# Three low parts of weights and one of an activation change engine or place at the borders of a Mamba2 mixer

## What is computed

```
hx = modulate(rmsnorm(x, pre_norm[l, 0]), mx[0], mx[1])       # scale and shift by column
z, xbc, dt_raw = jnp.split(h @ w_in, ...)                     # mixer in: xs, b, c, z, dt
xbc = silu(dwconv1d(xbc, conv_w, conv_b))
acs = cumsum(dt * a)                                          # by chunk, both directions
y = (y + d_skip * xs) * silu(z); y = y * rsqrt(mean(y * y) + EPS)
y = y * norm_w; out = y @ w_out                               # mixer out
x = x + mx[2] * rmsnorm(out, post_norm[l, 0])
hx = modulate(rmsnorm(x, pre_norm[l, 1]), mx[3], mx[4])       # and so to the FFN
x = x + mx[5] * rmsnorm((silu(conv(hx @ w_a)) * (hx @ w_v)) @ w_down, post_norm[l, 1])
```

## Time and profile before

| what | value |
|---|---|
| time of the kernel, median of 3 runs | 1337.94 us (1337.78 to 1338.17) |
| time of the profiled execution | 1337.82 us |
| its span in the profile | 1336.1 us |
| PE busy | 1297.3 us (97%), with the matmuls of `stay_busy` in it |
| DVE busy | 876.5 us (66%) |
| ACT busy | 656.1 us (49%) |
| POOL busy | 334.4 us (25%) |
| mean granted clock of the PE | 0.998 |

### The profile page before, as it was taken

How to read it: one execution, slowest core, us unless ns; L and a number is a source line. 1 busy time by engine, 2 the same in 40 slices (tenths; PEclk the granted TensorE clock), 3 DMA queues, 4 the chain that set the end, 5 groups by cost and what they waited for, 6 DMA issues and landing times. The chain is left out here.

```text
span 1336.1 us, 22159 instructions
## 1 busy us (share of the span) xinstructions
PE 1297.3 (97%) x8454; PEld 1093.4 (82%) x8454; DVE 876.5 (66%) x1717; ACT 656.1 (49%) x1037; POOL 334.4 (25%) x236
## 2 busy tenths in 40 slices
PE   5999999999999999999999999999999999999997
PEld 2678888887767888888888867899898879899997
DVE  4678777777697644222445778777777877774675
ACT  4445544445356433322333365555555645674664
POOL 1000000000203755105553030210111230683772
PEclk9999999999999999999999999999999999999999
DMA  9643444335470632234324334533333348366753
GB/s 345 202 142 123 131 132 137 127 118 167 158 244 23 190 95 87 71 110 123 98 71 134 103 126 111 158 95 95 95 95 94 95 157 255 110 200 173 219 164 111
DMA packets 274794, 183.28 MB, mean 137 GB/s; under 512 B 6642, under 2 KB 249106, under 8 KB 274706
## 3 DMA queue, kind: packets, MB, share of 16 engines
q1 hardware_dynamic: 274162, 180.00, 44.7%
q10 hardware_dynamic: 544, 2.10, 0.4%
HBM read 181.03 MB, written 1.05 MB: 136 GB/s over the span
## 5 line engine op out<-in xcount | busy, mean ns | idle before, releaser
L2218 PE MATMUL bank<-hh,wh 128*128 128x512 f32 (+1 forms) x1298 | 456.3, 352 | 3.5 <-DVE wl L1394 1.6
L2220 PE MATMUL bank<-hh,wl 128*128 128x512 f32 (+1 forms) x1298 | 451.6, 348 | 0.0
L2219 PE MATMUL bank<-hl,wh 128*128 128x512 f32 (+1 forms) x1298 | 451.2, 348 | 0.0
L849 ACT ACTIVATE wh<-wraw 128x1024 fp32r<-128x1024 f32 (+2 forms) x265 | 256.9, 985 | 84.0 <-PE bank L2220 59.4
L2218 PEld LDWEIGHTS bank<-hh,wh 128*128 128x128 f32 x1298 | 244.0, 188 | 39.1 <-DVE wl L1394 3.5
L1868 DVE SCALAR_TENSOR_TENSOR conv<-bank,pv,conv 128x189 f32<-128x189 f32 (+3 forms) x396 | 172.4, 436 | 152.9 <-ACT conv L1126 138.0
L2220 PEld LDWEIGHTS bank<-hh,wl 128*128 128x128 f32 x1298 | 243.9, 188 | 32.5
L1394 DVE TENSOR_TENSOR wl<-wraw,wh 128x1024 fp32r<-128x1024 f32 (+2 forms) x171 | 192.9, 1149 | 116.9 <-ACT wh L849 116.9
L2219 PEld LDWEIGHTS bank<-hl,wh 128*128 128x128 f32 x1298 | 244.1, 188 | 30.1
L737 POOL TENSOR_TENSOR wl<-wraw,wh 128x1024 fp32r<-128x1024 f32 (+2 forms) x87 | 198.8, 2291 | 197.3 <-ACT wh L849 197.0
L783 POOL TENSOR_TENSOR hl<-yT,hh 128x512 fp32r<-128x512 f32 x13 | 19.5, 1522 | 352.8 <-DVE gates L1764 340.3
(11 more groups left out here) (354 smaller groups left out, 2069.0 us busy)
## 6 DMA issues: line engine op xcount, KB each, us to landing
wraw<-in_ffn_w_up SPq DMA_DIRECT2D x88, 512.0 KB, 3.9
araw<-in_ada_w SPq DMA_DIRECT2D x40, 1024.0 KB, 8.2
wraw<-in_mb_w_in SPq DMA_DIRECT2D x48, 512.0 KB, 4.0
wraw<-in_hg_w_in SPq DMA_DIRECT2D x40, 512.0 KB, 3.9
wraw<-in_ffn_w_down SPq DMA_DIRECT2D x32, 512.0 KB, 4.0
wraw<-in_mb_w_out SPq DMA_DIRECT2D x16, 512.0 KB, 4.8
gates<-in_ada_w SPq DMA_DIRECT2D x5, 1024.0 KB, 9.3
wraw<-in_hg_w_out SPq DMA_DIRECT2D x8, 512.0 KB, 4.2
```

The costliest lines, as they stand in the source:

```text
L849: act.activation(slot(whp, n, 0, size), wraw[:, n % SLOTS, 0:size], ACT.Copy).then_inc(w_hi, 1)
L2218: pe.matmul(dst, W, hi(k), start=(k == 0), stop=False, **skip)
L2219: pe.matmul(dst, W, lo(k), start=False, stop=False, **skip)
L2220: ins = pe.matmul(dst, L, hi(k), start=False, stop=(k == nk - 1), **skip)
```

## The change

It has four parts.

1. The low part of `b 0` at border one is made by POOL (`part(at["b", 0])`, between `split_rest(0, T)` and `norm_low(1, T)`) instead of by DVE behind tile 1.
2. The low part of `xs 1 1` is made by DVE right behind the six scans of `dt_sums`, instead of behind all of `dt_sums`.
3. At the mixer's end DVE copies `yt 7` instead of ACT, with `tensor_scalar`, and makes the last tile's low part instead of POOL. The copies stand ahead of `gate_scales(1, 0)`, the low part behind it.
4. The low part of `up 1 0 1 1` at border two is made by POOL, between `y_low(1, ...)` and `norm_low(2, SEQ)`, instead of by DVE behind tile 1.

```diff
--- before.py
+++ after.py
@@ -432,7 +432,7 @@
         if g == MB_GROUPS + 1:
             plan.add(("am", LATE + 9), 6, "act")
         if Q:
-            mkey(("yt", q), "act")
+            mkey(("yt", q), "act" if q < MB_GROUPS - 1 else "dve")
         if S:
             mkey(("off", p, 0), "dve")
             mkey(("off", p, 1), "dve")
@@ -492,7 +492,7 @@
             for c in range(nf):
                 for part in range(2):
                     sub(("up", l, half, c, part), SUB, P, cols(a["ffn_w_up"][l], 0, KT, part * FF + (f0 + c) * P, P),
-                        ffp[l, half, "up"][0] + 2 * c + part + 1, "dve" if half == 0 and 2 * c + part < 5 - l or by_vector(l, half, c, part) else "pool")
+                        ffp[l, half, "up"][0] + 2 * c + part + 1, "dve" if half == 0 and 2 * c + part < 5 - 2 * l or by_vector(l, half, c, part) else "pool")
             for m in range(KT):
                 done = plan.index[("fy", l, m)][0] if half else ffp[l, 0, "down"][0] + m + 1
                 for j, (k0, nk) in enumerate(((0, KT), (KT, nf - KT))):
@@ -507,7 +507,7 @@
     for g in range(MB_GROUPS):
         for i in range(2):
             sub(("xs", g, i), SUB, P, cols(m_in, 0, KT, XS0 + (2 * g + i) * P, P), ("xs", g, i))
-        sub(("b", g), SUB, P, cols(m_in, 0, KT, B0 + g * P, P), ("b", g))
+        sub(("b", g), SUB, P, cols(m_in, 0, KT, B0 + g * P, P), ("b", g), "dve" if g else "pool")
         sub(("c", g), SUB, P, cols(m_in, 0, KT, C0 + g * P, P), ("c", g))
         for i in range(2):
             sub(("z", g, i), SUB, 256, cols(m_in, 4 * i, 4, 256 * g, 256), ("z", g))
@@ -801,6 +801,7 @@
         y_low(0, range(2, KT - 1))
         norm_low(0, T)
         split_rest(0, T)
+        part(at["b", 0])
         norm_low(1, T)
 
         pool.wait_ge(x_new, KT + 1)
@@ -828,7 +829,8 @@
             pool.wait_ge(skc_ready, g + 1)
             pool.tensor_tensor(hd(skip[:, :, :], 2), hd(xtok[:, 0:2, :], 2),
                                skc[:, :, :].unsqueeze(3).to_broadcast([P, 2, 4, HD]), ALU.mult).then_inc(scaled_ready, 1)
-        y_low(1, range(KT))
+        y_low(1, range(KT - 1))
+        part(at["up", 1, 0, 1, 1])
         norm_low(2, SEQ)
         split_rest(1, SEQ)
 
@@ -1329,7 +1331,7 @@
                 split_hi(at["z", g, 0] + 3)
             if g == MB_GROUPS + 1:
                 ada_rows(LATE + 9)
-            if Q:
+            if 0 <= q < MB_GROUPS - 1:
                 key = ("yt", q)
                 plan.wait_ready(act, key)
                 yk = yT[:, :, :].rearrange("p a b -> p (a b)")
@@ -1484,7 +1486,7 @@
             step.wait()
             V.tensor_scalar(ssx[:, 0:n], ssx[:, 0:n], 0.0, None, ALU.max).then_inc(var_ready, 1)
 
-        def add_and_norm(l, s, n, rows, weight=None):
+        def add_and_norm(l, s, n, rows):
 
             i = 2 * l + s
             first, second = ("r", l, s), ("r2", l, s)
@@ -1530,8 +1532,6 @@
                     plan.empty(ins, "dve", second)
                 if m < KT - 1 and (m == 0 or n == T):
                     turn(m + 1)
-                if m == 1 and weight is not None:
-                    split_lo(weight)
             hhn[0] += KT
 
         xn, rn, norms = [0], [0], [0]
@@ -1942,7 +1942,7 @@
         psum_freed_dve = plan.freed["dve"]
         ffn_dve(0, T, True)
         variance(0, 1, T, at["b", 0] - 1)
-        add_and_norm(0, 1, T, LATE + 5, at["b", 0])
+        add_and_norm(0, 1, T, LATE + 5)
 
         u, e, w = dtw[:, 0, :], dtw[:, 1, :], dtw[:, 2, :]
 
@@ -1985,6 +1985,7 @@
                         step(ins)
                     ends.append((r, slice(lo, hi), hi - 1 if d == 0 else lo))
             ins.then_inc(dt_dve, 1)
+            split_lo(at["xs", 1, 1])
             dve.wait_ge(dt_dve, 3)
             for r, c, last in ends:
                 step(V.tensor_scalar(elf[r, c], atf[r, c], -1.0, atf[r, last:last + 1], ALU.mult, ALU.add))
@@ -2151,7 +2152,8 @@
                 if g == 0:
                     ada_add(LATE + 6)
                     dt_sums()
-                split_lo(at["z", g, 0] + 3)
+                else:
+                    split_lo(at["z", g, 0] + 3)
             if S:
 
                 for d in range(2):
@@ -2174,8 +2176,16 @@
                 for j in range(2):
                     split_lo(at["z", g, 0] + 4 + j)
         hhn[0] += KT
+        key, k = ("yt", MB_GROUPS - 1), KT - 1
+        plan.wait_ready(dve, key)
+        for f in range(2):
+            ins = V.tensor_scalar(yT[:, k, f * 256:(f + 1) * 256], bank[plan.bank(key)][:, f * 256:(f + 1) * 256],
+                                  prm("mb_norm", 2 * k + f), None, ALU.mult)
+        plan.empty(ins, "dve", key)
         step.wait()
         gate_scales(1, 0)
+        dve.wait_ge(hh_ready, 5 * KT)
+        V.tensor_tensor(hl[:, k, :], yT[:, k, :], hh[:, k, :].bitcast(F32), ALU.subtract).then_inc(yl_ready, 1)
         step.wait()
         for m in range(KT):
             if m == 0:
@@ -2193,7 +2203,7 @@
             if m == 4:
                 ada_add(LATE + 10)
         variance(1, 0, SEQ, at["up", 1, 0, 1, 0])
-        add_and_norm(1, 0, SEQ, LATE + 11, at["up", 1, 0, 1, 1])
+        add_and_norm(1, 0, SEQ, LATE + 11)
         ffn_dve(1, SEQ, False)
         dve.wait_ge(rstd_ready, rn[0] + 1)
         plan.wait_emptied(dve, ("xr", 1, 1))
```

## The result

The changed kernel takes 1341.39 us (median of 13 runs, 1339.34 to 1342.55); the kernel before takes 1337.99 (13 runs). The ratio is 1.0025, 95% interval 1.0018 to 1.0032: slower by 3.4 us. The sum was +1.5. One of the 13 runs, at 1339.34, is the forecast; the profiled one took 1341.14, with a span of 1339.4.

The account below looks back on a forecast made before the run. The PE, busy for 97% of the span, bounds the kernel, with a chain on ACT and DVE at each border. The terms 1.7 - 0.1 - 0.6 + 0.5 make +1.5 us, median 1339.4, range 1336.6 to 1341.4.

Parts of the forecast that it names:

- The sum: Whole kernel: 1.7 - 0.1 - 0.6 + 0.5 = +1.5 us, a median of 1339.4, given 68%.
- Part 1, +1.7: Border one: POOL's low part holds DVE's L1483, tile 0's first matmul moves from 783.85 to 785.7; +1.7 us.
- the weight load's idle: Border one: 0.41 us of idle bounds tile 2's lateness; less the usual distance of loads, removing L1394 gains 0.1.
- the rival: Both borders: the PE's idle of about 2.3 us lets its clock fall; one fall gives 1341.1; 12%.
- Part 2, -0.1: Mixer's start: L2804's 1.4 us wait moves to cd, which needs bank 6; -0.1 us, bounds 0 and -1.4.
- Part 3, -0.6: Mixer's end: DVE's copies and low part replace ACT's and POOL's; -0.6 us, bounds -0.4 and -0.9.
- Part 4, +0.5: Border two: POOL holds L1485, tile 0 moves by 1.7, tile 7 comes at 1150.3, not 1149.77; +0.5 us.
- The open question: Border two: L1485, with one SBUF input, taken as held; the rival that it is not gives 1337.7; 10%.
- The price: One clock fall loses 1.7 us, taken from the trace's fall near the start, 0.66 on average over 5 us.
- The range: Whole kernel: 1336.6 to 1341.4, leaving out a double clock fall and most of the case without any hold.
- the double fall: The clock falling twice, left out of the range; one fall was priced at 1.7 us.

Follow-up runs that it names:

- parts 2 and 3 alone: The kernel before with parts 2 and 3 of the change, both borders as before: 1338.37 us, ratio 1.0002.
- the one with both gates: The changed kernel with GpSimd waiting for the variance before the low parts of b 0 and up 1 0 1 1: 1337.02 us, ratio 0.9991.
- fewer fillers: The kernel before with 10 instead of 18 filler matmuls at border one and 8 instead of 16 at border two: 1338.35 us, ratio 1.0005.
- part 1 and part 4 alone: Two kernels, each the kernel before with one part of the change: part 1, 1339.41 us (1.0016); part 4, 1338.67 us (1.0007).
- more fillers: The changed kernel with 27 instead of 18 filler matmuls at border one and 25 instead of 16 at border two: 1340.52 us, ratio 1.0018.
- three new places: Changed kernel, GpSimd waiting for the variance, z 1 0's low part moved behind cb's readings (1335.43 us), behind dt_by_token (1338.17) or into DVE's pause (1334.60).

## Why the prediction was right or wrong

- **Part 1, +1.7.** Measured +1.67 at tile 0 and, with L1394's place behind tile 1, +1.4; the removed instruction was worth 0.25 and not 0.1, since I took only the weight load's idle. The hold of 2.52 us (2.5 forecast) and the first matmul at 785.5 (785.7) came as worked out; the idle was 2.1 us where the rival has 2.3.
- **Part 2, -0.1.** Measured 0.0, and as forecast in kind: the 1.4 us went to cd, and bank 6 held it there. What I did not ask is what the PE does around the new place of the wait.
- **Part 3, -0.6.** Measured -0.58; two `tensor_scalar` of 128x256 take 0.88 us where I had 0.80.
- **Part 4, +0.5.** Measured +0.43 by itself. The open question, whether a maximum with one SBUF input is held, is answered: it is, 2.40 us in both profiles. The Trainium skill, "SBUF — State Buffer", section "Who interferes with whom", says so of an operation in a two-port mode, and the trace agrees: L1487 ends at 1140.63, 0.16 us behind POOL's L737.
- **The sum.** +1.5 forecast, 1.41 + 0.01 - 0.58 + 0.43 = +1.27 measured. It describes the fastest of the 13 runs, 1339.34, and not their median. The mean granted clock on record falls as the time rises: 0.998 in that run, 0.9952 on average in the six from 1340.32 to 1341.39, 0.9938 in the six from 1342.16 to 1342.55, where one fall takes 0.0013.
- **The step that failed** is the weight of the rival, "no pause later lowered it, though none was this long", at 12%. A trace in which no idle is as long as the new one says nothing against a fall, and the sum made two such idles. The price was sound: 1.7 forecast, 1.55 measured where the PE is the bound (border one), and 0.6 where it soon waits for tiles (border two: +0.99 in place of +0.43). With the sum these make the 3.4 us of the table. The row from which the price was taken shows no such loss itself: three profiles without a fall at the start (the changed kernel, parts 2 and 3 alone, the one with both gates) reach 773 us only 0.05 to 0.13 us sooner, so the 1.7 us hold only where the PE is the bound. The third place, cd, I did not see at all. There a wait of the old length, moved behind thin work, is followed by a fall in about half of the executions, if the upper heaps are read as above; of four profiles with this wait one has the fall.
- The range held the median by 0.01 us, and by luck: it reached so far only to take in one fall, and the +3.4 us are the +1.3 of the sum and a loss to the clock of 2.1 us, in the profiled run from the double fall that the range was meant to leave out.

What decides in which execution the clock falls stays open. An idle of 2.05 to 2.23 us ahead of tile 0 stands in six places of the profiles (two of the changed kernel, two with fewer fillers, one each of part 1 and part 4 alone), and a fall followed in three of them. In the 22 other passages of a border in the 14 profiles, with an idle of at most 0.44 us ahead of tile 0, none did; this, more than the one profile with more fillers, ties the fall to the idle. I tried nothing that would fix the moment.

## What to carry to other kernels

- Price a stall twice: the time of the wait, and the clock behind it. Filler matmuls have to be counted anew whenever a chain beside them gets longer; nine more, 0.22 to 0.23 us apart, closed the idle here.
- When GpSimd takes over work from VectorE, let it start behind VectorE's last operation that needs two SBUF operands or, like the maximum here, is done in SBUF faster than an addition of the same size (0.29 and 0.43 us), and while VectorE reads PSUM. One wait for a semaphore that was there already, at each border, turned +3.4 us into -0.9 (medians).
- Followed to the next engine, a wait tells where a piece of work is free. The same 1.2 us on DVE cost 0.9 us, 2.0 us or 0.1 in three new places, and the free place was visible in the trace as an idle of 1.57 us with GpSimd idle too. Look at the spread of the runs as well as the median: two heaps 1.5 us apart were, by all that the profiles show, one event that comes in about half of the executions.

## What the runs showed of the hardware

- The granted clock halved for 3.4 us behind idles of 1.46 us (after thin transposes), 1.9, 2.05, 2.11 and 2.23 us, and in other executions did not. Matmuls of 512 columns then step by 0.427 us instead of 0.23.
- A held DVE instruction ends with POOL's plus its own time less 0.14 us: POOL ends at 778.88, L1485 at 779.43.
- What such a fall costs depends on the waits behind it: 1.55 us at border one, 0.6 or nothing at border two, 1.4 at cd.
